# A hybrid decoder step on one core: 192 prompt tokens meet all experts in streamed blocks, 64 tokens and the sample keep gathered rows

## The chip, the cores and the metric

The kernel runs on one core of one Trainium2 chip. The metric is the device time of an execution in microseconds. The kernel before took 1012.31 us (median of three runs, 1011.79 to 1012.58).

## The reference, cut to what matters

One step of a one-layer decoder: 256 prompt tokens and 8 x 4 sample tokens go through two attention mixers and then through a channel mixer (PEER) with 16,384 single-neuron experts. Everything is float32. The change is in the channel mixer:

```python
D_MODEL, PEER_HEADS, PEER_NKEYS, PEER_TOPK = 1024, 8, 128, 16      # 128 * 128 experts
q = (xc @ w_pq).reshape(c, PEER_HEADS, 2, PEER_HALF)
s = jnp.einsum('chpd,hpkd->chpk', q, sub_keys)
sv, si = lax.top_k(s, PEER_TOPK)
cand = (sv[:, :, 0, :, None] + sv[:, :, 1, None, :]).reshape(c, PEER_HEADS, -1)
cid = (si[:, :, 0, :, None] * PEER_NKEYS + si[:, :, 1, None, :]).reshape(c, PEER_HEADS, -1)
cv, ci = lax.top_k(cand, PEER_TOPK)
eid, gate = jnp.take_along_axis(cid, ci, axis=-1), jax.nn.softmax(cv, axis=-1)
act = jax.nn.gelu(jnp.einsum('chkd,cd->chk', u_emb[eid], xc), approximate=False)
return jnp.einsum('chk,chkd->cd', gate * act, v_emb[eid])
```

Each token picks 8 x 16 = 128 experts. An expert has a row of 1,024 numbers in `peer_u` (dotted with the token) and one in `peer_v` (added to the output with weight gate x gelu). Both tables hold 16,384 rows of 4 KB.

## The kernel before, in words

The tokens are three tiles: prompt tile 0 and prompt tile 1 (128 tokens each) and the sample, tile 2 (32 tokens). Each tile runs through its heads (`heads_part`, `post`), its attention (`prompt` for tiles 0 and 1, `sample` for tile 2), the output projection (`wo_product`), the query product and the choice of experts (`query_product`, `best_keys`, `choose`). Its experts then are work in the background of the next tile's front.

Expert work is cut into slots. A slot is one chosen expert for 128 partitions: 64 tokens x 2 for a prompt tile, 32 tokens x 4 for the sample, so that the tiles have 128, 128 and 32 slots (`SLOTS`). For each slot POOL issues two indirect gathers of 128 rows of 4 KB, one of `peer_u` (L1996) and one of `peer_v` (`fetch_v`, L1978). DVE takes the 1,024-long dot products (`dot_slot`, L1453), ACT turns two slots at a time into weights (`gelu_slot`: gelu L1092, gate L1094, spread over a 64-column diagonal L1101), and PE adds weight x `peer_v` row into `acc` (`sum_slot`, through the helper `mm`, L463). Rings of seven to nine tiles hold the gathered rows.

The order is written by hand. Class `Experts` holds, for each of PE, ACT and DVE, how many slots are due: every `share(w)` or `advance(w)` in the program text adds a weight, and the engine runs the slots that are due at that point, before the next step of the front. All engines are in order, so a slot that waits holds what stands behind it. 40 slots are done while tile 0 still chooses (`EARLY`), 88 during the front of tile 1, 128 during that of tile 2, and the sample's 32 at the end. Results are normalised by `finish(t)` after `y_root(t)`. SP loads weights, cache pages (`step_pages`, `index_pages`) and stores outputs in one list.

Tile 0's token matrix for PE is `xt[0]`; `bank0` to `bank3` are four PSUM banks taken in turn; `acc` and `xr_even` fill the other four.

Of the kernel before, what the change touches and what calls it, by code (L numbers as in the profile page):

```python
# [15 lines left out]
U32 = mybir.dt.uint32  # L16
I32 = mybir.dt.int32
ALU = mybir.AluOpType
# [43 lines left out]
GELU_LAG, SUM_LAG, V_LAG = 3, 6, 5  # L62
# [5 lines left out]
CHOOSE, EARLY = 2, 40  # L68
PRELOADED = 4
SLOTS = [128, 128, 32]  # L70
BASE = [sum(SLOTS[:t]) for t in range(3)]
FRONT = 5 * W_IN + 4 * W_HEADS + 8 * W_PQ + 16 * CHOOSE

SHARES = [16 * CHOOSE, FRONT + 12 + 9 * W_PROMPT, FRONT - 8 * CHOOSE + 3 * W_INDEX + 2 * STEPS * sum(W_MID.values())]
PARTS = [[(0, 1), (1, 1), (2, 2), (4, 2), (6, 2)], [(2 * c, 2) for c in range(4)], [(0, 1), (1, 1)]]
STARTS = [[16 * h for h, _ in p] for p in PARTS]
CHOSEN = [sum(len(p) for p in PARTS[:t]) for t in range(3)]
U_GUESTS = [(24, 118), (144, sum(SLOTS) - 1)]
U_PLACE, U_LAST, U_USE = [], [], []
for n in range(sum(SLOTS)):  # L80
    places = [*range(RU), *(RU + i for i, (a, b) in enumerate(U_GUESTS) if a <= n <= b)]
    last = {p: max([m for m in range(n) if U_PLACE[m] == p], default=-1) for p in places}
    U_PLACE.append(min(places, key=lambda p: (last[p], p)))
    U_LAST.append(last[U_PLACE[n]])
    U_USE.append(U_PLACE[:n].count(U_PLACE[n]))
N_SLOTS = sum(SLOTS)
V_PLACE = [n % RV for n in range(N_SLOTS)]
V_USE = [n // RV for n in range(N_SLOTS)]
V_LAST = [n - RV for n in range(N_SLOTS)]
END_X, END_GUEST, END_ROW = N_SLOTS - 5, N_SLOTS - 4, N_SLOTS - 1  # L90
V_END = {END_X: RU, END_GUEST: RU + 1, END_ROW: U_PLACE[N_SLOTS - 7]}
for i, n in enumerate(V_END):
    V_PLACE[n], V_USE[n] = RV + i, 0
for n in (N_SLOTS - 3, N_SLOTS - 2):
    V_LAST[n] = n - RV - 2
    V_PLACE[n], V_USE[n] = V_LAST[n] % RV, V_LAST[n] // RV + 1
STAIR = 16 + 15 * 8
FIRST_SLOT = [0, EARLY, 128, 256]
# [7 lines left out]
def build(nc, inp, cst, out, scr_b, scr_d, scr_s, scr_z1, scr_z2):  # L106
    ctx = ExitStack()
    with ctx:
# [18 lines left out]
        g_q = sb("g_q_sb", [128, QL])  # L127
        g_kv = sb("g_kv_sb", [128, KVL])
# [12 lines left out]
        x = [x_b[t % 2] for t in range(3)]  # L141
        xr_odd = sb("xr_odd", [128, DM])
        more_v = sb("more_v", [128, DM])
        eid = [sb(f"eid{t}", [128, SLOTS[t]], U32) for t in range(3)]
        gate = [sb(f"gate{t}", [128, SLOTS[t]]) for t in range(3)]
# [10 lines left out]
        u_ring = [first_u[:, :], more_u[:, :]] + [rows[:, i, :] for i in range(5)] + [b[:, :] for b in x_b]  # L156
        v_ring = [more_v[:, :]] + [rows[:, i, :] for i in (5, 6, 7, 8, 9, 10, 11, 12)]
        v_ring += [u_ring[p] for p in V_END.values()]
# [3 lines left out]
        wts = sb("wts", [128, RC])  # L162

        wflat = sb("wring", [128, NW * 8 * CW])
        zflat = sb("z", [128, 2048])
# [4 lines left out]
        xt = [xt_f[:, 0:8 * P[t]].rearrange("p (k n) -> p k n", k=8) for t in range(3)]  # L170
        mix_f = sb("mix_t", [128, 1024])
        xn2 = mix_f
# [3 lines left out]
        qq_t = sb("qq_t", [QKD, NH, 128])  # L176
        qn_t = sb("qn_t", [128, HR, 128])
# [90 lines left out]
        z1_kept = xr_odd[:, 0:512]  # L268
# [13 lines left out]
        xr = [xr_even[:, :], xr_odd[:, :]]  # L282
# [29 lines left out]
        class Signal:  # L312
# [11 lines left out]
            def wait(self, eng, step):  # L324
                eng.wait_ge(self.sem, self.at[step] * self.unit)

        tiles = [0, 1, 2]
        first_in = sem("first_consts_in")
# [11 lines left out]
        y_out = sem("y_stored")  # L340
        w_in_slot = [sem(f"w_slot{i}_in") for i in range(4)]
# [30 lines left out]
        ROOTS = [("x", 0), ("x", 1), ("x", 2), ("z", 0), ("h", 0), ("z", 1), ("h", 1), ("z", 2), ("y", 0), ("h", 2), ("y", 1),  # L372
                 ("y", 2)]
        square_ready = Signal("mean_square_ready", [r for r in ROOTS if r[0] != "y"])
        root_ready = Signal("root_ready", ROOTS)
        first_pair_scored = sem("first_two_heads_of_a_quad_scored")
# [33 lines left out]
        u_in = [sem(f"u{i}_in") for i in range(RU + 2)]  # L410
        v_in = [sem(f"v{i}_in") for i in range(RV + len(V_END))]
# [3 lines left out]
        y_ready = Signal("y_ready", tiles)  # L415
        y_square = Signal("square_sums_of_sample_y_ready", [2])
# [3 lines left out]
        class Experts:  # L420
# [4 lines left out]
            def __init__(self, name, slot, lag):  # L425
                self.slot, self.lag, self.done, self.n = slot, lag, 0, 0
                self.log = handovers[name] = []

            def front(self, t):
                self.t, self.weight = t, 0  # L430

            def share(self, w):
                if self.t:
                    self.advance(w)

            def advance(self, w):
                self.weight += w
                self.log.append((self.t, w))
                assert self.weight <= SHARES[self.t], (self.t, self.weight)
                first, end = FIRST_SLOT[self.t:self.t + 2]  # L440
                until = first + (end - first) * self.weight // SHARES[self.t] - self.lag
                while self.n < until:
                    self.slot(max(self.t - 1, 0), self.n)
                    self.n += 1

            def closer(self, lag):
                first, end = FIRST_SLOT[self.t:self.t + 2]
                self.rest(self.t - 1, first + (end - first) * self.weight // SHARES[self.t] - lag - BASE[self.t - 1])

            def rest(self, t, slots=None):  # L450

                while self.n < BASE[t] + (slots or SLOTS[t]):
                    self.slot(t, self.n)
                    self.n += 1
# [14 lines left out]
        def _(pe):  # L469
# [41 lines left out]
            def sum_slot(t, n):  # L511

                if n % PAIR < PAIR - 1:
                    return
                m, u = P[t], n // PAIR
                if u == BASE[t] // PAIR:
                    if t:
                        y_ready.wait(pe, t - 1)
                    else:
                        z1_kept_done.wait(pe, 3)  # L520
                    for c in range(2 if t < 2 else 0):
                        mm(acc[0:m, c * 512:(c + 1) * 512], ident[0:m, 0:m], x[t][0:m, c * 512:(c + 1) * 512], True, False)
                    for q in range(0 if t < 2 else 4):
                        mm(acc[32 * q:32 * q + 32, 0:256], ident[0:32, 0:32], x[t][0:32, 256 * q:256 * q + 256], True, False)
                pe.wait_ge(spread_done, u + 1)
                for v in range(u * PAIR, u * PAIR + PAIR if t < 2 else 0):
                    pe.wait_ge(v_in[V_PLACE[v]], (V_USE[v] + 1) * 16)
                for c in range(2 if t < 2 else 0):
                    for j in range(PAIR):
                        g, m = WIDE * j, WIDE  # L530
                        i = mm(acc[g:g + m, c * 512:c * 512 + 512], spread[u % RD][:, j, 0:m],
                               v_ring[V_PLACE[u * PAIR + j]][:, c * 512:c * 512 + 512], False, False)
# [34 lines left out]
            def heads_part(t):  # L567

                n, r0 = P[t], ROW0[t]
                if t == 1:  # L570
                    experts.closer(4)
# [1748 lines left out]
```

## Time and profile before

| | before |
|---|---|
| median of three runs | 1012.31 us |
| profiled execution, span from first to last instruction | 1080.4 us |
| busy PE / DVE / ACT / POOL | 742.8 / 686.7 / 404.0 / 622.1 us |
| bytes moved by DMA | 381.54 MB, mean 353 GB/s |
| mean granted TensorE clock | 0.819 of 2.4 GHz |

The span is the only time that the profile gives for the profiled execution; it is 68.1 us (6.7%) above the median of the runs. A granted clock of 1.00 is 2.4 GHz and 0.50 is 1.2 GHz; a value between is the mean over a stretch. One float32 product on PE leaves two matmul records and two weight loads in the trace. Times of a window view are busy times in that window; the DMA share is the mean busy share of the core's 16 DMA engines and can read slightly over 1.

### The profile page before, as it was taken

The page shows a single profiled execution, that of the slowest core. Times are in us where ns is not written, and L with a number is a line of the kernel's source. Part 1 is how long each engine was busy: PE and PEld are TensorE (multiplying, and loading weights), DVE is VectorE, ACT ScalarE, POOL GpSimd, SP SyncE. Part 2 cuts the span into 40 slices and gives each one's busy share as a digit, 9 for nine tenths or more (in the row PEclk, how much of TensorE's full clock was granted, in tenths as well). Part 3 has the DMA queues.
Part 4 walks back from the last instruction along what each step waited for, and adds up shares of the span by engine and source line. Part 5 has one row for each costly group of instructions (what it writes and reads, how often), then busy time and mean ns, then how long its engine had stood idle before and what let it go on. Part 6 is the DMA issues. An engine that isn't in the chain of part 4 may idle for free.

```text
span 1080.4 us, 13828 instructions
## 1 busy us (share of the span) xinstructions
PE 742.8 (69%) x4217; PEld 379.1 (35%) x4217; DVE 686.7 (64%) x1725; ACT 404.0 (37%) x1154; POOL 622.1 (58%) x584
## 2 busy tenths in 40 slices
PE   8999986554798677766536768757637567765444
PEld 3575834111354435543212233323213235231111
DVE  1363776997288543698695559988974535639542
ACT  1162142332356470333223346354516742322412
POOL 0000275777667765475565656766775665667664
PEclk9999997877778899988867878877778878887656
DMA  9924699999979999999899999999998999999997
GB/s 364 331 79 184 217 349 411 411 360 377 336 252 359 348 400 412 398 379 379 278 314 325 373 388 353 391 362 362 407 412 308 411 417 416 414 411 409 382 376 270
DMA packets 122443, 381.54 MB, mean 353 GB/s; under 512 B 16026, under 2 KB 40682, under 8 KB 117122
## 3 DMA queue, kind: packets, MB, share of 16 engines
q0 software_dynamic: 83696, 304.81, 74.0%
q1 hardware_dynamic: 38578, 75.78, 19.2%
q8 instruction: 34, 0.56, 0.2%
q14 instruction: 39, 0.32, 0.1%
q10 hardware_dynamic: 96, 0.07, 0.0%
HBM read 378.16 MB, written 4.14 MB: 354 GB/s over the span
## 4 chain that ended last, share of the span: by engine, by line
PE 28%; DVE 19%; issue 17%; ACT 10%; another core or an unknown queue 9%; DMA 8%; POOL 6%; SPq 3%; ACTq 0%; POOLq 0%; DVEq 0%
PE bank L463 17%; PE acc L463 9%; DVE rows L1453 6%; DMA w_uq_sb<-in_w_uq 3%; PE bank L466 3%; POOL rows L1978 3%; DMA rows<-in_peer_v,eid 2%; POOL rows L1996 2%; ACT spread L1101 2%; ACT L1092 1%; SPq L2069 1%; DVE shared L1793 1%; DVE shared L1782 1%; ACT shared L1063 1%
## 5 line engine op out<-in xcount | busy, mean ns | idle before, releaser
L463 PE MATMUL acc<-rows,spread 128*64 128x512 f32 (+1 forms) x1124 | 329.3, 682 | 143.9 <-ACT spread L1101 51.9
L1978 POOL DMA_INDIRECT rows<-in_peer_v,eid x254 | 275.8, 1086 | 160.5 <-issue 66.6
L1996 POOL DMA_INDIRECT rows<-in_peer_u,eid x184 | 193.2, 1050 | 109.0 <-issue 54.7
L463 PEld LDWEIGHTS acc<-rows,spread 128*64 128x64 f32 (+1 forms) x1124 | 89.1, 156 | 310.3 <-issue 240.2
L1453 DVE CUSTOM_DVE_ANT_0 rows<-rows,xr_even 128x1024 f32<-128x1024 f32 x89 | 108.1, 1218 | 34.0 <-DMA rows<-in_peer_u,eid 26.4
L1453 DVE CUSTOM_DVE_ANT_0 rows<-rows,xr_odd 128x1024 f32<-128x1024 f32 x95 | 116.2, 1223 | 19.6 <-DMA rows<-in_peer_u,eid 18.8
L1101 ACT ACTIVATE spread<-wide_consts,wts 128x64 f32<-128x64 f32 (+1 forms) x288 | 83.7, 337 | 35.2 <-remote 25.0
L1996 POOL DMA_INDIRECT first_u<-in_peer_u,eid x37 | 38.2, 1032 | 101.5 <-DVE eid L1835 81.6
L463 PE MATMUL acc<-more_v,spread 128*64 128x512 f32 (+1 forms) x140 | 73.6, 695 | 18.9 <-ACT spread L1101 9.9
L1094 ACT ACTIVATE wts<-gelus,gate 128x1 f32<-128x1 f32 x288 | 69.1, 287 | 4.7
L1063 ACT ACTIVATE shared<-bank 128x512 f32<-128x512 f32 (+4 forms) x68 | 27.8, 456 | 76.3 <-remote 35.5
L1092 ACT ACT_TABLE_LOAD x42 | 53.9, 1283 | 0.7
L1092 ACT ACTIVATE gelus<-dots 128x2 f32<-128x2 f32 x144 | 28.4, 197 | 65.4 <-issue 44.0
L1978 POOL DMA_INDIRECT more_v<-in_peer_v,eid x32 | 35.5, 1108 | 19.9 <-issue 8.5
L1996 POOL DMA_INDIRECT more_u<-in_peer_u,eid x37 | 40.0, 1082 | 11.3 <-issue 11.0
L466 PE MATMUL bank<-ident,shared 128*128 128x128 f32 (+4 forms) x162 | 28.2, 292 | 26.2 <-issue 7.2
L1453 DVE CUSTOM_DVE_ANT_0 x<-x,xr_even 128x1024 f32<-128x1024 f32 x30 | 36.5, 1217 | 8.9 <-DMA x<-in_peer_u,eid 8.6
L1748 DVE MAX8 small<-ql_t 32x8 f32<-32x1056 f32 x32 | 39.9, 1248 | 0.8
L1996 POOL DMA_INDIRECT x<-in_peer_u,eid x30 | 34.3, 1144 | 9.6 <-issue 9.6
L1749 DVE MATCH_REPLACE8 ql_t<-small,ql_t 32x1056 f32<-32x1056 f32 x32 | 39.4, 1230 | 0.0
L463 PE MATMUL bank<-xt,wring 128*128 128x128 f32 x256 | 35.3, 303 | 5.1 <-issue 4.4
L463 PEld LDWEIGHTS bank<-xt,wring 128*128 128x128 f32 x256 | 34.0, 217 | 11.9 <-issue 10.9
(278 smaller groups left out, 1222.4 us busy)
## 6 DMA issues: line engine op xcount, KB each, us to landing
wring<-in_w_pq SPq DMA_DIRECT2D x12, 1024.0 KB
z<-in_w_pq SPq DMA_DIRECT2D x5, 1024.0 KB, 4.8
wring<-in_cache_ckv SPq DMA_DIRECT2D x40, 128.0 KB
rows<-in_w_in SPq DMA_DIRECT2D x2, 2048.0 KB, 15.2
rows<-in_w_pq SPq DMA_DIRECT2D x2, 2048.0 KB, 8.3
wring<-in_w_out SPq DMA_DIRECT2D x4, 1024.0 KB
wring<-in_cache_kv SPq DMA_DIRECT2D x32, 128.0 KB
rows<-in_peer_v,eid POOLq DMA_INDIRECT x254, 7.5
```

What stands on the lines that cost most here:

```text
L463: return T.matmul(o, lhsT=l, rhs=r, start=start, stop=stop, skip_group_check=True)
L466: return T.transpose(o, i, ident[0:i.shape[0], 0:i.shape[0]])
L1063: c = A.activation(o, i, ACT.Copy, scale=scale)
L1092: link(A, A.activation(gelus[:, k:k + PAIR], dots[:, k:k + PAIR], ACT.Gelu))
L1094: g = A.activation(wts[:, k + i:k + i + 1], gelus[:, k + i:k + i + 1], ACT.Copy, scale=gate[t][:, n - BASE[t] - PAIR + 1 + i:n - BASE[t] - ...
L1101: g = A.activation(spread[u % RD][:, i, 0:m], sel[:, 0:m], ACT.Copy, scale=wts[:, k + i:k + i + 1])
L1453: V.tensor_tensor_reduce(out=u, in0=u, in1=xr[j], scale=1.0, scalar=0.0, op0=ALU.mult, op1=ALU.add, accum_out=dots[:, k:k + 1]).then_inc(d ...
L1748: link(V, V.max(small[0:32, 24:32], i_s))
L1749: link(V, V.match_replace(out=i_s, in_to_replace=small[0:32, 24:32], in_values=i_s, imm_value=TAKEN))
L1782: V.max_index(index[j][:, 0:8], values[j][:, 0:8], score[j])
L1978: nc.gpsimd.indirect_dma_start(out=v_ring[V_PLACE[n]], out_offset=None, in_=inp["peer_v"], in_offset=bass.IndirectOffsetOnAxis(ap=eid[t][: ...
L1996: nc.gpsimd.indirect_dma_start(out=u_ring[U_PLACE[n]], out_offset=None, in_=inp["peer_u"], in_offset=bass.IndirectOffsetOnAxis(ap=eid[t][: ...
```

## The change

Tile 0 is split. Its first 64 tokens keep gathered slots: 128 experts x 64 tokens on 128 partitions are 64 slots (`FEW`). The other 64 tokens of tile 0 and all 128 of tile 1 (`MANY` = 192) are multiplied with all experts. The experts are 128 blocks of 128; SP streams a turned copy of `peer_u` (`peer_ut`) and `peer_v`, 512 KB each per block. PE multiplies the block with the 192 tokens (`dots_of_blocks`), ACT takes gelu of two blocks at a time (`gelu_blocks`), DVE multiplies with a dense gate matrix (`weigh`), and PE adds the block's rows into two accumulators (`sums_of_blocks`). The sample keeps 32 gathered slots, now last on POOL.

The dense gate matrix holds 32 blocks at a time (`g_part`, four parts in two buffers). It is made in 24 chunks of 8 tokens per part: for each token a one-hot matrix of its experts' first key times the gate (`one_i`, by DVE) and one of the second key (`one_j`, by POOL; for the odd chunks of the first part by DVE), multiplied on PE (`turn_weights`) and copied out by ACT (`keep_weights`). The chosen indices and gates are first turned so that experts lie on partitions (`turn_chosen`, `keep_chosen`).

The schedule becomes one list of items: 32 pairs of gathered slots of tile 0, 48 pairs of blocks, then 16 pairs of blocks alternating with 16 pairs of the sample's slots. 8 items are due while tile 0 chooses, 20 during the front of tile 1, 4 in the heads of tile 2; then come the first 24 chunks, and 48 pairs of blocks during the sample stage. SP runs the same list two items ahead for the loads. `y` of tile 0 leaves in two halves.

```diff
-SLOTS = [128, 128, 32]
+FEW, ALL = 64, 128
+MANY = 128 + ALL - FEW
+N_SLOTS = FEW + NB * NT
+BLOCKS = 128
+PBLOCKS, PCHUNKS = 32, MANY // 8
+MIX_FROM = 48
+ITEMS = [("s", u) for u in range(FEW // PAIR)] + [("d", d) for d in range(MIX_FROM)]
+for d in range(MIX_FROM, BLOCKS // PAIR):
+    ITEMS += [("d", d), ("s", FEW // PAIR + d - MIX_FROM)]
+D0, N_ITEMS = FEW // PAIR, len(ITEMS)
+FIRST_ITEM = [0, 8, 28, D0, D0 + MIX_FROM]
+def chunks_of(d):
+    p, k = d // (PBLOCKS // PAIR), d % (PBLOCKS // PAIR) - 4
+    return range(PCHUNKS * (p + 1) + 2 * k, PCHUNKS * (p + 1) + 2 * k + 2) if k >= 0 and p < BLOCKS // PBLOCKS - 1 else range(0)
...
+            def turn_weights(c):
...
+                b = take(pe, ("g", c))
+                for k in range(8):
+                    i = mm(b[:, 32 * k:32 * k + 32], one_j[c % 2][:, k, :], one_i[c % 3][:, k, :])
+                full(i, ("g", c))
+            def dots_of_blocks(d):
+                b = take(pe, ("u", d))
+                for j in range(PAIR):
+                    n = PAIR * d + j
+                    pe.wait_ge(du_in[n % 4], (n // 4 + 1) * 16)
+                    u = bias_u[0] if n % 4 == 3 and n >= KEYS_TO else dense_u[n % 4]
+                    for k in range(8):
+                        i = mm(b[:, MANY * j:MANY * j + MANY], u[:, 128 * k:128 * k + 128], xd[:, k, :], k == 0, k == 7)
+                full(i, ("u", d))
+            def sums_of_blocks(d):
+                pe.wait_ge(weights_ready, d + 1)
+                for j in range(PAIR):
+                    n = PAIR * d + j
+                    pe.wait_ge(dv_in[n % 4], (n // 4 + 1) * 16)
+                    v = bias_u[1] if n % 4 == 3 and n >= KEYS_TO else dense_v[n % 4]
+                    w = acts[d % 4][:, MANY * j:MANY * j + MANY]
+                    for q in range(2):
+                        mm(acc_d[64 * q:64 * q + 64, :], w[:, 0:64], v[:, 512 * q:512 * q + 512], False, False)
+                    for q in range(2):
+                        i = mm(acc_1[:, 512 * q:512 * q + 512], w[:, 64:192], v[:, 512 * q:512 * q + 512], False, False)
+                i.then_inc(dense_done, 1)
+            def step(n):
...
+                if kind == "d":
+                    for c in chunks_of(k):
+                        turn_weights(c)
+                    dots_of_blocks(k)
+                sums(n - BEHIND)
...
+            def gelu_blocks(d):
+                if d >= 4:
+                    act.wait_ge(dense_done, d - 3)
+                b = ready(act, ("u", d))
+                A.activation(acts[d % 4], b[:, 0:PAIR * MANY], ACT.Gelu).then_inc(acts_ready, 1)
+                act.wait_ge(acts_ready, d + 1)
+                drained(A.activation(small[:, 41:42], small[:, 14:15], ACT.Copy), ("u", d))
...
+                link(V, V.tensor_tensor(o, free(iota[:, PBLOCKS * p:PBLOCKS * p + 1], (0, 8), (1, PBLOCKS)),
+                                        free(t[:, 0, 0:1], (1, 8), (0, PBLOCKS)), ALU.is_equal))
+                V.tensor_tensor(o, o, free(t[:, 2, 0:1], (1, 8), (0, PBLOCKS)), ALU.mult).then_inc(one_i_ready, 1)
+                if c < PCHUNKS and c % 2:
...
+                    V.tensor_tensor(one_j[1], free(iota[:, 0:1], (0, 8), (1, 128)), free(t[:, 1, 0:1], (1, 8), (0, 128)),
+                                    ALU.is_equal).then_inc(one_j_first, 1)
...
+                dve.wait_ge(acts_ready, d + 1)
+                V.tensor_tensor(acts[d % 4], acts[d % 4], g_part[p % 2][:, PAIR * MANY * k:PAIR * MANY * (k + 1)],
+                                ALU.mult).then_inc(weights_ready, 1)
...
                 else:
+                    experts.rest(D0)
+                    for c in range(PCHUNKS):
+                        turn_weights(c)
+                    start_sums_of_tile_1()
+                    experts.front(3)
                     sample()
...
+            fetch(0, FEW)
...
+            for c in range(BLOCKS // PBLOCKS * PCHUNKS):
+                k = c % PCHUNKS
+                if c < PCHUNKS and c % 2:
+                    continue
+                if c >= 2:
+                    ready(pool, ("g", c - 2))
...
+                for q in range(8):
+                    i = nc.gpsimd.tensor_scalar(one_j[c % 2][:, q, :], iota, t[:, q:q + 1], None, ALU.is_equal)
+                i.then_inc(one_j_ready, 1)
+            fetch(FEW, N_SLOTS)
...
+                if n >= 4:
+                    ready(sp, ("u", (n - 4) // PAIR))
...
+                load(o, inp["peer_ut"][n, :, :], du_in[n % 4])
...
+                if n >= 4:
+                    sp.wait_ge(dense_done, (n - 4) // PAIR + 1)
...
+                load(o, inp["peer_v"][128 * n:128 * n + 128, :], dv_in[n % 4])
```

## Rows read from the trace of the kernel before

**Rows 1.** The page: busy time of each engine, and the queue of the gathers.

```profile
PE 742.8 (69%) x4217; PEld 379.1 (35%) x4217; DVE 686.7 (64%) x1725; ACT 404.0 (37%) x1154; POOL 622.1 (58%) x584
...
q0 software_dynamic: 83696, 304.81, 74.0%
```

**Rows 2.** Windows: stretch, length; busy PE, PEld, DVE, ACT, POOL; clock, DMA share, GB/s.

```profile
0.00:109.00 109.00, 101.82 (x564) 61.45 (x565) 39.75 (x116) 33.07 (x88) 3.34 (x8) 0.98 0.67 241
109.00:245.00 136.00, 96.60 (x563) 54.42 (x561) 108.97 (x391) 43.54 (x117) 86.19 (x79) 0.87 0.92 348
245.00:445.00 200.00, 151.22 (x691) 88.88 (x692) 107.19 (x219) 89.40 (x247) 128.63 (x123) 0.84 0.95 357
445.00:550.00 105.00, 63.79 (x355) 35.08 (x356) 89.22 (x342) 31.25 (x91) 64.43 (x61) 0.82 0.95 350
550.00:602.00 52.00, 26.65 (x119) 10.71 (x117) 31.69 (x80) 14.67 (x55) 32.96 (x29) 0.76 0.96 331
602.00:893.00 291.00, 194.66 (x1139) 81.78 (x1137) 209.49 (x354) 139.60 (x376) 192.54 (x175) 0.79 1.00 381
893.00:985.00 92.00, 63.68 (x503) 32.31 (x499) 53.16 (x150) 26.49 (x88) 58.44 (x53) 0.82 1.02 413
985.00:1080.40 95.40, 44.36 (x298) 14.43 (x294) 47.22 (x76) 26.00 (x95) 55.61 (x60) 0.63 0.92 353
```

**Rows 3.** Windows, expert sums alone (tile spread): busy PE, PEld, ACT; clock, DMA, GB/s.

```profile
245.00:445.00 200.00, 63.84 (x224) 17.96 (x225) 17.42 (x60) 0.84 0.95 357
445.00:550.00 105.00, 38.12 (x138) 10.29 (x140) 9.00 (x31) 0.82 0.95 350
...
602.00:893.00 291.00, 98.72 (x344) 25.93 (x344) 26.42 (x90) 0.79 1.00 381
893.00:985.00 92.00, 36.24 (x120) 9.60 (x122) 8.22 (x28) 0.82 1.02 413
```

**Rows 4.** Windows, dot products alone (L1453, two instructions per dot): busy DVE; clock, DMA, GB/s.

```profile
109.00:245.00 136.00, 47.63 (x80) 0.87 0.92 348
245.00:445.00 200.00, 68.85 (x114) 0.84 0.95 357
445.00:550.00 105.00, 34.47 (x58) 0.82 0.95 350
550.00:602.00 52.00, 16.34 (x28) 0.76 0.96 331
```

**Rows 5.** Timeline of PE: start, length; a query product, and two expert sums of one moment.

```profile
119.67 7.41 PE L463 MATMUL bank<-xt,rows 128*128 128x128 f32 x64
...
154.92 0.59 PE L463 MATMUL acc<-more_v,spread 128*64 128x512 f32 x1
154.93 0.59 PE L463 MATMUL acc<-rows,spread 128*64 128x512 f32 x1
```

**Rows 6.** Timeline of weight loads: first and tenth of a run of 512-column products.

```profile
139.91 0.19 PEld L463 LDWEIGHTS acc<-rows 128*128 128x128 f32 x1 [0.24 <-issue]
...
143.77 0.19 PEld L463 LDWEIGHTS acc<-rows 128*128 128x128 f32 x1 [0.24 <-issue]
```

**Rows 7.** Groups on DVE by shape: busy us, mean ns of one; idle before.

```profile
L1499 DVE TENSOR_TENSOR shared<-shared 128x256 f32<-128x256 f32 x4 | 1.7, 425 | 0.1
...
L1696 DVE COPY shared<-bank 128x128 f32<-128x128 f32 x8 | 2.3, 291 | 22.1 <-remote 18.4 <-PE bank L463 3.7
```

**Rows 8.** Groups on POOL by shape: busy us, mean ns of one; idle before.

```profile
L1996 POOL DMA_INDIRECT rows<-in_peer_u,eid x184 | 193.2, 1050 | 109.0 <-issue 54.7 <-DVE dots L1453 45.4 <-PE bank L463 8.8
...
L2299 POOL MEMSET const-float32-0.0<- 128x1 f32 x1 | 0.1, 98 | 0.2 <-issue 0.2
```

**Rows 9.** Groups on ACT by shape: busy us, mean ns of one; idle before.

```profile
L1092 ACT ACT_TABLE_LOAD x42 | 53.9, 1283 | 0.7
...
L1063 ACT ACTIVATE shared<-bank 128x512 f32<-128x512 f32 x32 | 16.8, 597 | 18.0 <-remote 14.4 <-PE bank L466 3.6
```

**Rows 10.** Timeline of DVE: the root of tile 0's result in `finish`.

```profile
579.59 0.16 DVE L1506 RECIPROCAL small<-small 128x1 f32<-128x1 f32 x1 [9.69 <-ACT small L1129]
```

More of the change, by code:

```diff
@@ L79 @@
[L79 to L88, printed above, removed]
@@ L442, in advance, with rest @@
+            def rest(self, until):
                 while self.n < until:
[L443 to L453, printed above, removed]
+                    self.step(self.n)
@@ L542, in _ @@
+            experts = Experts("PE", step, 0)
             share = experts.share
@@ L1387, in _ @@
                 else:
+                    experts.rest(D0)
+                    for c in range(PCHUNKS):
+                        keep_weights(c)
+                    experts.front(3)
                     sample()
@@ L1467, in _, with step @@
+            def step(n):
+                kind, k = ITEMS[n]
+                if n == NORM_0A:
+                    finish("0a")
+                if kind == "s":
+                    for j in range(PAIR):
+                        dot(PAIR * k + j)
+                weigh(n - 1)
+                for c in chunks_of(ITEMS[n + 1][1]) if n + 1 < N_ITEMS and ITEMS[n + 1][0] == "d" else []:
+                    one_hots(c)
+            experts = Experts("DVE", step, 0)
             share = experts.share
@@ L2110, in _, with load_gain @@
+            def load_gain(o, m):
+                w = DM * m // 128
+                for q in range(128 // m):
+                    load(o[m * q:m * q + m, :], bass.AP(inp["g_final"].tensor, inp["g_final"].offset + w * q, [[0, m], [1, w]]), g_fin_in)
             load(relb, inp["rel_bias"], hot_in)
@@ new lines, in _ @@
+            experts.front(3)
+            experts.rest(D0 + 2)
+            for e in range(3):
+                if e:
+                    ready(sp, ("is", e - 1, 1))
+                    step_pages("m", e)
+                share(W_INDEX)
+            for e in range(STEPS):
+                for i in range(2):
+                    share(W_MID["m"])
+                ready(sp, ("mso", e))
+                if e + 3 < STEPS:
+                    step_pages("m", e + 3, step_ids(e + 3) if e + 3 >= SUB else None)
+                if e == 4:
@@ L2211, in _ @@
+            sp.wait_ge(sample_scored, 2)
+            load(gains[1], bcast(inp["g_final"], DM), g_fin_in)
+            load_gain(gains["0b"], 64)
+            load_gain(gains[2], 32)
+            experts.rest(N_ITEMS)
+            for n in range(BLOCKS - 4, BLOCKS):
+                load_v(n)
+            for t in (1, "0b", 2):
+                output(t)
+            sp.wait_ge(y_out, 16 * 9)
             sp.wait_ge(stored_z, 240)
+            assert handovers["SP"] == [w for w in handovers["PE"] if w[0] == 3]
```

620 lines of the change are left out of this document (380 added, 240 removed).

## The prediction, made before the changed kernel was run

> **What bounds the kernel now.** I read the page first, for what is busy over the whole span: no engine is above 69%, and the queue of the gathers alone keeps the 16 DMA engines busy for 74% [rows 1]. Then I cut the span where the program changes stage (109 us: first keys of tile 0; 245: heads of tile 1; 445: its first keys; 550: its last gates; 602: sample; 893: its output projection; 985: its last gates) and read each stretch [rows 2]. From 109 us on, the DMA engines are at 0.92 to 1.02 of their time while PE is at 46 to 76%. Only the first 109 us look otherwise: PE is busy for 101.82 of them. So the gathers set the pace: 288 slots of 2 x 512 KB are 302 MB of the queue's 304.81 MB [rows 1]. POOL, busy for 192.54 of 291 us in the sample stage, is second. PE has room, but a number to keep in mind is how much: 1080 minus 743 us, 338 us [rows 1].
>
> **What the change removes.** 192 of 288 slots: 201 MB of gathers, 384 POOL issues, 192 dots. It adds 128 x 2 x 512 KB = 134 MB of plain loads. DMA has 67 MB less to move of 381.5, which at the 381 GB/s of the sample stage [rows 2] is 176 us. That is the gain on the old bound, and it would be the whole story if PE had the room.
>
> **What it adds on PE.** The unit is a record; a product has two. Nine steps between the weight loads of 512-column products take 143.77 - 139.91 = 3.86 us, 0.429 us each [rows 6]; 64 records of 128 columns, each with its own 128x128 weights, take 7.41 us, 0.115 each [rows 5]. Both are at full clock, and a line through them gives 0.167 us for 192 columns. Two products with 64 columns of weights start 0.01 us apart and run side by side [rows 5]. So a block costs:
> - dots: 8 products of 192 columns, 16 x 0.167 = 2.67 us;
> - sums: the two 64-column products side by side are 2 records' time, the two 128-column ones 4: 6 x 0.429 = 2.57 us.
>
> 5.24 us a block, 671 us for 128. Already this is twice the room that PE has now.
>
> A gate chunk is 8 products of only 32 columns with fresh 128x128 weights. By the line a record would take 0.037 us if the weight load hid; no such record stands in the rows. The upper end is the 0.115 of a 128-column record with the same load. I take 0.115, since the load and not the columns should set the pace there: 1.84 us a chunk, 96 chunks 177 us (at 0.037, 57).
>
> **The sum, stage by stage, in the profiled execution's time.** Dense work cannot start before tile 1's experts are chosen, as the gates and the token matrix need them.
> - To 245 us: 16 dots instead of 40, at 47.63/40 = 1.19 us [rows 4] 28.6 us less on DVE, whose idle there is 136 - 109 = 27 us [rows 2]. Gain 28.6 to 55.6; I take the middle, 42: 203 us.
> - Tile 1's front, 305 us now: 86 slots' dots [rows 4] become 40. DVE: 196.4 - 103.3 + 47.6 = 141 us. PE: 215.0 - 102.0 + 20 pairs of 2.25 (362 records, 8 a pair, took 102.0 [rows 3]) = 158. Transfers: 0.95 x 305 less 46 slots of 1.05 MB at 355 GB/s (136 us) = 154. Lower end 158; upper end 305 - 46 x 1.19 = 250, where nothing but DVE's dots goes. Its steps depend on each other, so I take 200, near the middle: 403 us.
> - Heads of tile 2: 52 us now, less the wait of 9.69 for tile 0's result [rows 10], which moves into the sample stage behind dense items, and less 14 dots (16.34 [rows 4]), plus 8 dots: 36. 439 us.
> - First 24 chunks, with nothing of the sample beside them: PE 44 us. DVE: 48 x 0.425 [rows 7] + 12 of 1,024 elements at a dot's 1.2 = 35. POOL: 12 x 8 compares of 128 elements. The rows show no arithmetic on POOL; the ends are 0.098 (a memset of one column) and 1.05 (issuing a gather) [rows 8]. I take 0.3, by the same shape on DVE, 0.291 [rows 7]. POOL waits for the chunk two back, so building and multiplying alternate: 2.4 + 1.84 + some 0.6 of handovers, 12 times: 58 us (44 to 130). Dense work starts at 497 us.
> - From there PE: 671 + 72 chunks 132 + the sample's own PE work, 258.3 - 135.0 = 123 us at clock 0.8 [rows 2, 3], 99 at full clock + the sample's 32 slots, whose four 256-column products run side by side, 4 x 0.21 a pair, 14. Total 916 us. With no wait at all 916; at the 93% of the first stretch [rows 2] 981. I take 950: 1447 us.
> - Result: one root and product cost 9.69 + 1.3 us [rows 10]; three overlap in part. 11 to 33, I take 15: 1462 us.
>
> Against the profiled span of 1080.4 that is +382. The span is 68.1 us above the median. I assume that the excess lies where transfers set the pace and scale only the part before 497 us by 0.937: 466 + 950 + 15 = **1431 us** (all scaled 1370, nothing scaled 1462). I call it 1430.
>
> A rule against POOL's part: [rows 8] leave its price open by a factor of ten. The Trainium skill (GPSIMD Engine Reference, section 4.1) advises against elementwise work on GpSimd: about half as fast as VectorE with two inputs, near its rate with one. At twice 0.291 the first chunks would take 86 us in place of 58 and the time 1457. No run here shows it yet.
>
> **Costed at nothing, and the cover.** For a pair of blocks ACT needs a gelu of 384 columns (under 0.6 us), at most two table loads of 1.28 [rows 9] and two chunk copies, some 4 us; DVE a product of 384 (under 1.2) and four one-hots of 0.425 [rows 7], 3 us. Both lie beside 10.5 us of PE. If they were late, each wait would stand in PE's order in front of all sample work, as the sums wait for `weights_ready`; two items lie between, 20 us. SP's loads are 2.1 MB a pair, 200 GB/s against 381 reached [rows 2]; SP waits there for dots two pairs back, and the page loads and projection weights of the sample queue behind that wait, three steps ahead of use. In the last 16 items 2 slots come on top: 4.2 MB in 11.3 us, 370 GB/s, close to the 353 to 413 of the last stretches: 0 to 9 us. POOL starts the sample's gathers only after its last one-hot, at pair 47; pairs 48 and 49 cover the first landing. The outputs of tile 0 and the loads of `g_final` move on SP, a few transfers behind dense loads, covered by the same pairs.
>
> **The rivals.**
> 1. POOL is slow. If a compare costs the 1.05 us of an issue, the first chunks take 130 us (+72), and two chunks 17 us where their pair of blocks needs 10.5 + 3.7: 36 pairs x 2.6 = +95. About 1600 us. For it: no row has POOL arithmetic; against: 128 elements are little. It decides from 0.9 us on.
> 2. The clock sags. Now it is granted at 0.98 where PE is busy for 93%, 0.63 where it is for 46% [rows 2]. If waits of the sample's chain let the dense stretch swing between 1.2 and 2.4 GHz as the whole kernel does now, at 0.82, PE's 916 us become 1117: 1600 to 1640. Against: dense items are long and independent. The Trainium skill (TensorE: Matmul & The Clock Gate, Part 1) has the array at half clock unless activity releases it, and by that rule gaps between bursts bring this case about.
> 3. The other side: dense products overlap as the 64-column ones do, or cost one record. Dots, sums and chunks at half price: 402 + 99 + 14 = 515 us, near what the transfers allow (168 MB of experts and, by the loads in the code, some 30 of pages and weights: 520 us at 381 GB/s): 466 + 520 + 15 = 1001 us, 1.1% faster. It decides from 0.52 of my price on. Against: the 128-column weights of [rows 5, 6] run one record after another, without exception.
>
> **How the numbers follow.** Forecast 0.79, POOL 0.10, clock 0.08, the other side 0.03. The forecast's own range, since the ends of the stages before dense work (427 to 632 us together) hardly fall all to one side, is 1320 to 1540; to hold 8 in 10 with the slow cases I go to 1310 and 1600. A measurement tells some 0.2%. Faster has 0.02, the same 0.01 (the other side falling short), slower 0.97.
>
> **What would show it.** Right: PE busy over 90% from some 450 to 500 us to the end with a clock near 1; records of 192 columns every 0.167 us and 512 every 0.429; the DMA share near a half; 235 MB of expert bytes. The steps are wrong if dense work starts before 400 or after 580 us, if a chunk's record is far from 0.115, or if POOL's compares show before PE's waits. A span below 1200 us would break the price of a record, on which all rests.

## The result, and the profile after

The changed kernel takes **1599.33 us** (median of four executions, 1598.61 to 1602.31) beside 1012.16 us before: a ratio of 1.580, 95% interval 1.577 to 1.582. The prediction said 1430, with a range from 1310 to 1600: the side and the cause came out, and the time lies 0.7 us inside the end of the range, 169 us above the forecast. The profiled execution has a span of 1600.5 us and took 1602.31. In three experiments below with unused products, one or two executions lie 60 to 70 us from the others at another mean granted clock; they are named there.

The page of the profile, in the lines that answer to [rows 1]:

```profile
PE 1435.5 (90%) x8083; PEld 990.9 (62%) x8083; DVE 578.2 (36%) x1566; ACT 389.8 (24%) x905; POOL 618.9 (39%) x872
...
q1 hardware_dynamic: 76226, 211.65, 37.7%
q0 software_dynamic: 28400, 103.46, 17.9%
```

The gathers' queue has fallen from 74% of the DMA engines' time [rows 1] to 17.9%, and with the streamed tables all queues stay near 56%. PE is busy for 1435.5 us where it was for 743.

The windows by stage, as [rows 2] (tile 1's heads begin at 202 us, its last choice is at 428, the one-hots of the first chunk begin at 466, the dense blocks follow from 585 to 1590):

```profile
245.00:440.00 195.00, 131.63 (x689) 86.98 (x688) 111.86 (x389) 71.02 (x161) 49.41 (x52) 0.79 0.63 212
440.00:466.00 26.00, 18.30 (x86) 8.49 (x85) 10.87 (x22) 9.98 (x41) 14.87 (x16) 0.68 0.87 317
466.00:585.00 119.00, 87.10 (x393) 83.32 (x390) 36.57 (x71) 14.68 (x26) 73.71 (x102) 0.50 0.08 29
585.00:1130.00 545.00, 540.52 (x3096) 383.22 (x3096) 165.99 (x300) 137.17 (x268) 238.38 (x395) 0.96 0.47 160
1130.00:1360.00 230.00, 222.25 (x1430) 162.71 (x1430) 52.50 (x169) 36.03 (x74) 105.97 (x170) 0.95 0.48 176
1360.00:1590.00 230.00, 230.00 (x1152) 135.73 (x1150) 49.31 (x86) 32.72 (x119) 75.00 (x71) 0.99 0.83 306
```

From 585 us on PE is busy for 992.8 of 1005 us, as forecast, with the DMA share near a half up to 1360. The surprise is the stretch before it: 119 us in which the DMA engines stand still (0.08), PE is busy for 87 us, and the clock is at its lower level, 1.2 GHz. Against the prediction, stage by stage:

| step | predicted | after | difference |
|---|---|---|---|
| tile 1's heads begin | 203 | 202 | -1 |
| tile 1's front | 200 | 226 | +26 |
| heads of tile 2, to the first chunk | 36 | 38 | +2 |
| first 24 chunks | 58 | 119 | +61 |
| dense blocks, to the last product | 950 | 1005 | +55 |
| result | 15 | 10.5 | -4.5 |
| from the profile to the runs (the factor 0.937) | -31 | -1 | +30 |

The differences add up to +168.5. The experiments take the four large ones in turn. Inside the dense blocks, a pair of blocks and two chunks read like this at full clock (timeline of PE):

```profile
651.07 1.08 PE L506 MATMUL acc<-more_v,w_uq_sb 128*64 128x512 f32 x4
652.08 1.99 PE L506 MATMUL xr_even<-more_v,w_uq_sb 128*128 128x512 f32 x4
653.99 1.08 PE L506 MATMUL acc<-x,w_uq_sb 128*64 128x512 f32 x4
655.00 1.98 PE L506 MATMUL xr_even<-x,w_uq_sb 128*128 128x512 f32 x4
656.82 0.38 PE L509 MATMUL bank<-ident,shared 128*128 128x128 f32 x2
...
659.43 1.97 PE L506 MATMUL bank<-w_uq_sb,g_fin_sb 128*128 128x32 f32 x16
661.24 1.95 PE L506 MATMUL bank<-w_uq_sb,uk_t 128*128 128x32 f32 x16
```

Read the starts, since the ends are modelled and overlap. The sums of two blocks run from 651.07 to 656.82, 5.75 us where 2 x 2.57 = 5.14 were forecast. A chunk takes 1.81 (1.84 forecast). The dots of a pair take 5.40 (5.34 forecast), where no chunk stands right before them. But behind two chunks they look like this:

```profile
709.77 1.95 PE L506 MATMUL bank<-w_uq_sb,uk_t 128*128 128x32 f32 x16
711.56 4.53 PE L506 MATMUL bank<-xd,first_u 128*128 128x192 f32 x16
715.92 2.76 PE L506 MATMUL bank<-xd,more_u 128*128 128x192 f32 x16
718.62 1.08 PE L506 MATMUL acc<-more_v,w_uq_sb 128*64 128x512 f32 x4
```

The same 16 records take 4.36 us and then 2.70: for some microseconds the clock is at the lower level, with no gap in the work. After the low clock of the first chunks there are 13 such episodes, some 4 to 10 us each. Twelve stand at two chunks in a row, the last of them at 1370 us behind the last two chunks. One has no chunks near it: it begins at 1152 us, while PE waits 3.35 us for DVE between products of the sample:

```profile
1153.88 0.48 PE L509 MATMUL bank<-ident,shared 128*128 128x128 f32 x1 [3.35 <-DVE shared L1928]
```

### The profile page after: what moved, and what is told of

Same layout as the page of the kernel before. It is cut to its first block, busy times and chain, and to the rows that moved or that the text cites. A ratio compares the mean times of both kernels' runs of the same rounds, so it can differ in the third digit from the quotient of the medians.

```text
span 1600.5 us, 21795 instructions
## 1 busy us (share of the span) xinstructions
PE 1435.5 (90%) x8083; PEld 990.9 (62%) x8083; DVE 578.2 (36%) x1566; ACT 389.8 (24%) x905; POOL 618.9 (39%) x872
## 3 DMA queue, kind: packets, MB, share of 16 engines
q0 software_dynamic: 28400, 103.46, 17.9%
## 4 chain that ended last, share of the span: by engine, by line
PE 79%; DVE 5%; POOL 5%; DMA 5%; ACT 4%; issue 1%; SPq 0%; DVEq 0%; POOLq 0%; ACTq 0%
PE bank L506 49%; PE xr_even L506 16%; PE acc L506 13%; POOL g_fin_sb L2228 4%; DMA w_uq_sb<-in_w_uq 2%; PE bank L509 2%; DMA rows<-in_peer_v,eid 2%; DMA wring<-in_w_pq 1%; ACT L1209 1%; DVE shared L1988 0%; DVE shared L2002 0%; SPq L2236 0%; ACT L1371 0%; DVE rows L1624 0%; DVE shared L1999 0%
## 5 line engine op out<-in xcount | busy, mean ns | idle before, releaser
L2228 POOL TENSOR_SCALAR g_fin_sb<-wide_consts,g_q_and_g_kv 128x128 f32<-128x128 f32 x256 | 167.0, 671 | 221.6 <-PE bank L506 221.6
L506 PE MATMUL bank<-w_uq_sb,g_fin_sb 128*128 128x32 f32 x768 | 113.3, 307 | 32.8 <-POOL g_fin_sb L2228 31.9
L506 PEld LDWEIGHTS bank<-w_uq_sb,g_fin_sb 128*128 128x128 f32 x768 | 110.3, 227 | 46.4 <-POOL g_fin_sb L2228 35.1
L506 PE MATMUL bank<-w_uq_sb,uk_t 128*128 128x32 f32 x768 | 119.1, 316 | 0.0
L2228 POOL TENSOR_SCALAR uk_t<-wide_consts,g_q_and_g_kv 128x128 f32<-128x128 f32 x192 | 115.9, 629 | 0.0
L506 PEld LDWEIGHTS bank<-w_uq_sb,uk_t 128*128 128x128 f32 x768 | 115.2, 237 | 0.0
L506 PE MATMUL bank<-xd,x 128*128 128x192 f32 x512 | 108.3, 374 | 0.0
L2187 POOL DMA_INDIRECT rows<-in_peer_v,eid x88 | 83.2, 946 | 50.8 <-PE acc L506 29.8
L506 PEld LDWEIGHTS bank<-xd,x 128*128 128x128 f32 x512 | 99.3, 221 | 4.8 <-issue 4.8
L506 PE MATMUL bank<-xd,first_u 128*128 128x192 f32 x512 | 98.9, 350 | 0.0
```

The source lines that it names most:

```text
L506: return T.matmul(o, lhsT=l, rhs=r, start=start, stop=stop, skip_group_check=True)
L2187: nc.gpsimd.indirect_dma_start(out=v_ring[V_PLACE[n]], out_offset=None, in_=inp["peer_v"], in_offset=bass.IndirectOffsetOnAxis(ap=eid[:, a ...
L2228: i = nc.gpsimd.tensor_scalar(one_j[c % 2][:, q, :], iota, t[:, q:q + 1], None, ALU.is_equal)
```

## The experiments

Times are medians of four executions unless said otherwise. The ratios are to the kernel before on the same chip; a difference between two kernels is taken between their medians. The medians of the kernel before beside them lie between 1012 and 1014 us.

### Half of every dense dot

```diff
-                    for k in range(8):
-                        i = mm(b[:, MANY * j:MANY * j + MANY], u[...], xd[:, k, :], k == 0, k == 7)
+                    for k in range(4):
+                        i = mm(b[:, MANY * j:MANY * j + MANY], u[...], xd[:, k, :], k == 0, k == 3)
```

> Left out: in every dense dot product the products of the second 512 of 1,024 model columns (8 of 16 records a block). Theory (PE's price of float32 products sets the time from 585 us on): 128 blocks x 8 records x 0.168 us = 172 us less, of which some 5 come back in the last 32 blocks, where the transfers are at 0.83 of their time: 1430 us. Rival (transfers, or the order of gelu, weigh and sums, set the pace): 1590 to 1600 us, with PE's busy share falling instead. In between (1450 to 1480): the narrow gate products then weigh more and the clock is lower.

Measured: 1453.41 us (1449.52 to 1458.82), ratio 1.436 (1.430 to 1.441): 146 us less. In its profile the first chunks end at 585 us, as in the changed kernel, and the last product at 1443:

```profile
585.00:1443.00 858.00, 838.46 (x4664) 524.60 (x4668) 267.61 (x555) 206.07 (x462) 420.74 (x635) 0.94 0.64 231
```

PE is still busy for 838 of 858 us, so nothing else took over: the rival falls, and **PE's work sets the time**. Of the 172 us, 26 are missing, and most are found where the expectation's last sentence looked. The dots' own busy time fell by 156.5 us, from 374.4 to 217.9, and not by 172: the dots that run at the lower clock behind the chunks are a larger part of what is left (granted clock 0.94, before 0.96). PE's idle time rose by 7 us: PE now waits 4.8 us for rows of `peer_v` and 2.5 us for DVE's weighing, where the changed kernel has no such waits.

### Narrow sums first

```diff
+                pair = []
                 for j in range(PAIR):
...
+                    pair.append((w, v))
                     for q in range(2):
                         mm(acc_d[64 * q:64 * q + 64, :], w[:, 0:64], v[...], False, False)
+                for w, v in pair:
                     for q in range(2):
                         i = mm(acc_1[:, 512 * q:512 * q + 512], w[:, 64:192], v[...], False, False)
```

> Same work, other order: in the sums of a pair of blocks the 64-column products of both blocks come first, then the 128-column ones, so that the width of the weights changes twice in a pair and not four times. Theory (a change of width leaves a weight load in the open, and this is the excess of 2.92 us a block over 2.57): half of the changes goes, 64 pairs x 0.35 us = 22 us less: 1577 us. Rival (the excess has to do with other things, the bank of the accumulator or reading the weights): 1599 us.

Measured: 1579.01 us (1573.01 to 1581.63), ratio 1.560 (1.556 to 1.565): 20 us less. The timeline of PE:

```profile
649.31 1.08 PE L506 MATMUL acc<-more_v,w_uq_sb 128*64 128x512 f32 x4
650.22 1.03 PE L506 MATMUL acc<-x,w_uq_sb 128*64 128x512 f32 x4
651.17 1.99 PE L506 MATMUL xr_even<-more_v,w_uq_sb 128*128 128x512 f32 x4
653.00 1.88 PE L506 MATMUL xr_even<-x,w_uq_sb 128*128 128x512 f32 x4
654.71 0.38 PE L509 MATMUL bank<-ident,shared 128*128 128x128 f32 x2
```

5.40 us in place of 5.75 for the same products, and the second group of 128-column products starts 1.71 us before what follows it: four times the 0.429 of [rows 6], the price without the excess. So the excess belongs to the **change of width**. The accumulator changes at the same places; a change of accumulator without one of width was not run, but the step from one half of an accumulator to the other lies inside those 1.71 us and costs nothing. In the changed kernel's trace one sees why, in the weight loads (PEld) at such a change:

```profile
1588.12 0.30 PEld L506 LDWEIGHTS xr_even<-bias_d,w_uq_sb 128*128 128x128 f32 x2 [0.81 <-issue]
1588.13 1.98 PE L506 MATMUL xr_even<-bias_d,w_uq_sb 128*128 128x512 f32 x4
1588.66 0.19 PEld L506 LDWEIGHTS xr_even<-bias_d,w_uq_sb 128*128 128x128 f32 x1 [0.24 <-issue]
```

The first load of the new width starts with the product and not ahead of it, after 0.81 us of pause; within a width the next load starts while the product before it still runs, as in [rows 6].

### DVE alone makes the first one-hots

```diff
-                if c < PCHUNKS and c % 2:
-                    pe.wait_ge(one_j_first, c // 2 + 1)
+                if c < PCHUNKS:
+                    pe.wait_ge(one_j_first, c + 1)
...
-                if c < PCHUNKS and c % 2:
+                if c < PCHUNKS:
                     if c >= 2:
                         ready(dve, ("g", c - 2))
-                    V.tensor_tensor(one_j[1], ...
+                    V.tensor_tensor(one_j[c % 2], ...
...
-                if c < PCHUNKS and c % 2:
+                if c < PCHUNKS:
                     continue
```

In the changed kernel POOL and PE take turns (timeline, then PE's waits from 466 to 585 us):

```profile
481.42 3.62 PE L506 MATMUL bank<-w_uq_sb,g_fin_sb 128*128 128x32 f32 x16 [2.62 <-POOL g_fin_sb L2228]
...
484.85 3.60 PE L506 MATMUL bank<-w_uq_sb,uk_t 128*128 128x32 f32 x16
...
485.14 5.88 POOL L2228 TENSOR_SCALAR g_fin_sb<-wide_consts,chosen_of_tile_turned 128x128 f32<-128x128 f32 x8 [3.77 <-PE bank L506]
```

```profile
PE bank L506 <- POOL g_fin_sb L2228: 31.9, 12, 3.1
```

> Same work: the one-hot of the second key of the first 24 chunks is made by DVE alone, not by POOL and DVE in turn. Theory (POOL's 5.9 us a chunk and PE's two chunks at half clock alternate, and so make the first part 120 us long): DVE needs 2.1 us a chunk, PE 3.45 at half clock, so the part takes 24 x 3.45 = 83 us: 1562 us. Rival 1 (the clock is low there because PE waits): with the waits gone PE needs 1.84 us and DVE's 2.1 sets the pace, 50 us: 1530 us. Rival 2 (the copies out or the banks set the pace): 1599 us.

Measured: 1564.03 us (1559.13 to 1571.81), ratio 1.547 (1.540 to 1.554): 35 us less, the theory's number. Its windows before and over the first chunks, and PE's timeline:

```profile
450.00:466.00 16.00, 14.71 (x64) 7.13 (x64) 6.69 (x12) 5.14 (x23) 6.24 (x7) 0.50 1.04 391
466.00:550.00 84.00, 84.00 (x388) 82.76 (x387) 47.48 (x79) 14.71 (x24) 4.73 (x9) 0.50 0.09 33
```

```profile
480.01 3.60 PE L506 MATMUL bank<-w_uq_sb,g_fin_sb 128*128 128x32 f32 x16
483.42 3.60 PE L506 MATMUL bank<-w_uq_sb,uk_t 128*128 128x32 f32 x16
```

The waits are gone: PE is busy for 84.00 of 84 us. Yet a chunk still takes 3.41 us and the granted clock reads 0.50 all through, so rival 1, which had the low clock come from the waits in this part, falls as well. The clock is at 0.50 already when the part begins; what the chunks show here is that they do not raise it. At 1.81 the 24 chunks would take 43 us: once POOL's 35 us are gone, 38 us are lost to the clock.

### One chunk before the dots, one between them

```diff
-                    for c in chunks_of(k):
-                        turn_weights(c)
                     dots_of_blocks(k)
...
+                chunks = list(chunks_of(d))
+                if chunks:
+                    turn_weights(chunks[0])
                 b = take(pe, ("u", d))
                 for j in range(PAIR):
+                    if j and chunks:
+                        turn_weights(chunks[1])
```

> Same work, other order: of the two gate chunks of an item the second is multiplied between the dots of its two blocks, not right behind the first. Theory (two chunks in a row, 16 products of 32 columns, are what lets the clock fall for 3 to 10 us at a time between 690 and 1360 us): the episodes go, granted clock over 0.98 from 585 us on, some 30 us less: 1569 us. Rival 1 (one chunk of 8 products is enough): the episodes stay, 1599 us. Rival 2 (the episodes come from waits that only happen to lie there): 1599 us, and the dips move to other places than the chunks.

Measured: 1568.39 us (1566.66 to 1572.46), ratio 1.550 (1.546 to 1.555): 31 us less, for the same products in another order. The stretch with chunks, in the changed kernel and then in this one (whose window holds 71 records more), and this one's timeline:

```profile
591.00:1360.00 769.00, 756.77 (x4510) 543.69 (x4509) 218.00 (x469) 172.43 (x340) 338.39 (x554) 0.96 0.48 166
```

```profile
588.00:1340.00 752.00, 739.76 (x4581) 522.88 (x4581) 221.15 (x473) 175.56 (x345) 348.34 (x564) 1.00 0.50 175
```

```profile
704.28 1.87 PE L506 MATMUL bank<-w_uq_sb,g_fin_sb 128*128 128x32 f32 x16
705.98 2.85 PE L506 MATMUL bank<-xd,first_u 128*128 128x192 f32 x16
708.66 1.87 PE L506 MATMUL bank<-w_uq_sb,uk_t 128*128 128x32 f32 x16
710.37 2.85 PE L506 MATMUL bank<-xd,more_u 128*128 128x192 f32 x16
```

The twelve episodes at the chunks are gone: granted clock 1.00, and the dots behind a chunk take 2.68 us, not 4.36. Two chunks in a row let the clock fall; one between wider products did not in this kernel. Rival 1 falls. Rival 2 falls for those twelve, as PE's waits in this stretch are the same in both (12.2 us); it holds for the thirteenth, which stays: behind the same wait for DVE, now 3.36 us, the clock is at 0.50 from 1127 to 1133 us.

### Places for gathered rows up to slot 56

```diff
-CLEAR, GUEST = 40, 24
+CLEAR, GUEST = 56, 24
```

In the changed kernel, between 202 and 428 us, PE and POOL waited for this (the longest waits of PE, then of POOL):

```profile
PE acc L506 <- DMA rows<-in_peer_v,eid: 37.9, 7, 12.6
```

```profile
POOL more_u L2206 <- DVE dots L1624: 53.7, 5, 23.8
```

> Same work: the places of gathered rows that the gate matrix takes over are used up to slot 56, not 40, so that the slots of tile 1's front keep eight places. Theory (that front takes 226 us and not 200 as POOL waits for one of three places, and PE for the rows that POOL could not ask for: 37.9 us in 7 waits): most of the 26 us goes: 1575 us, the last choice of tile 1 near 404 us. Rival (DVE's dots or the chain of the front set its pace): 1595 to 1600 us. Against both: the first copies of the gate matrix wait for a later slot, up to 5 us.

Measured: 1574.00 us (1570.52 to 1577.04), ratio 1.551 (1.548 to 1.555): 25 us less. The last step of tile 1's choice, in the timelines of DVE of the changed kernel and of this one:

```profile
427.81 0.15 DVE L2063 COPY small<-small 128x1 f32<-128x1 f32 x1
```

```profile
405.83 0.15 DVE L2063 COPY small<-small 128x1 f32<-128x1 f32 x1
```

So the theory holds: 22 of the 26 us came from the **three places** that slots 40 to 63 were left. The waits are a chain: POOL may not ask for the next `peer_u` rows before DVE has used a place, the request for the `peer_v` rows stands behind that one in POOL's order, and PE holds the front of tile 1 until they land. With eight places PE has no waits for these rows left in tile 1's front.

### The four edits together

> The four edits that keep the work (narrow sums first, DVE's one-hots in the first part, split chunks, places up to slot 56) together. If each acts on a part of its own: 1599 - 20 - 35 - 31 - 24 = 1489 us. If two of them paid for the same time (split chunks and narrow sums both touch the clock), 1500 to 1520. Still far above the kernel before: PE's own work is then some 1,330 us.

Measured: 1485.83 us (1483.61 to 1486.23), ratio 1.465 (1.462 to 1.467): 113.5 us less, where the four alone gave 20.3 + 35.3 + 30.9 + 25.3 = 111.8. So they hardly overlap. It is the fastest of the changed kernels that do only the work that is needed, and 46% slower than the kernel before.

### Unused wide products in the first chunks

The low clock of the first 24 chunks is left. Four kernels put products of 256 columns between them, whose results go to the unused half of the bank:

```diff
                 for k in range(8):
                     i = mm(b[:, 32 * k:32 * k + 32], one_j[c % 2][:, k, :], one_i[c % 3][:, k, :])
+                    if c < PCHUNKS and k == 7:
+                        i = mm(b[:, 256:512], ident[:, :], xd_f[:, 0:256])
```

With two a chunk the condition is `k % 4 == 3`, with three `k in (2, 4, 7)`.

> Added to the kernel in which DVE makes all one-hots of the first 24 chunks (1564 us): behind each of these chunks one product of 256 columns whose result is not used (two records, 0.44 us at full clock). There PE is busy without a gap at a granted clock of 0.50, so waits are not what keeps it low. Theory A (32-column products leave the clock low, and a wide one between them lets it rise): a chunk takes 1.84 + 0.44 = 2.3 us, 55 instead of 82: 1537 us. Theory B (the clock stays low): 3.45 + 0.88 = 4.3 us, 104 us: 1586 us.

Measured: 1585.94 us (1577.52 to 1588.26), ratio 1.561 (1.556 to 1.566): 22 us more than without the products, theory B. The windows of its first chunks:

```profile
490.00:520.00 30.00, 30.00 (x128) 28.74 (x128) 14.04 (x22) 4.29 (x7) 0.00 (x0) 0.50 0.00 1
```

> As the kernel with one unused product of 256 columns behind each of the first 24 chunks, but with two, one behind each four products. Theory A: 1.84 + 0.88 = 2.7 us a chunk, 65 instead of 82: 1547 us. Theory B (the clock stays low): 3.45 + 1.76 = 5.2 us, 125 us: 1607 us. If the kernel with one product stays low and this one rises, it is the share of wide work that decides.

Measured, five executions: 1536.96, 1541.77 and 1543.98 us at a mean granted clock of 0.934 to 0.936, and 1604.67 and 1608.05 us at 0.895. These are the two theories' numbers, 1547 and 1607, from one and the same kernel; the profiled execution was the one of 1608.05, with a clock of 0.50 before and over the first chunks, which begin at 464 us:

```profile
450.00:464.00 14.00, 12.55 (x56) 6.27 (x54) 5.93 (x12) 5.13 (x23) 4.45 (x5) 0.50 1.04 393
464.00:585.00 121.00, 121.00 (x475) 112.52 (x474) 47.04 (x79) 14.10 (x23) 2.63 (x5) 0.50 0.06 20
```

The ratio of the three is 1.518 (1.515 to 1.522).

> The kernel with the four edits together (1486 us) and two unused products of 256 columns in each of the first 24 chunks. With that much wide work the earlier kernel ran at either level of the clock: three executions near 1541 us, two near 1606. So here too: at full clock 24 x (3.41 - 2.72) = 17 us less, 1469 us; at half clock 24 x 1.76 = 42 us more, 1528 us. Rival (the level is set by what went before the part, and that is another thing here): all executions at one of the two.

Measured, six executions: five from 1464.14 to 1467.14 us and one of 1525.61; ratio of the five 1.446 (1.442 to 1.450). Again both numbers (1469, 1528) were met, but the full clock more often. The profile is of one at full clock; its window over the first chunks:

```profile
440.50:503.00 62.50, 62.50 (x474) 60.04 (x472) 47.22 (x77) 14.17 (x23) 1.05 (x2) 1.00 0.15 51
```

The four edits alone, where the same part begins at the same time:

```profile
440.50:443.00 2.50, 2.50 (x23) 2.50 (x24) 2.27 (x4) 0.48 (x1) 0.00 (x0) 1.00 1.06 321
445.00:520.00 75.00, 75.00 (x353) 75.00 (x353) 43.75 (x73) 13.41 (x22) 3.23 (x6) 0.50 0.08 29
```

Without the wide products the part begins at full clock, falls during its second chunk and stays low to its end: 79 us. With them it stays at full clock: 64 us. So **more work makes the kernel faster** in five of six executions: 1466 us against 1486, with 48 products that nobody uses.

> As the kernel with two unused wide products a chunk, but with three. If the share of wide work decides the level: full clock in all executions, 24 x (3.41 - 3.16) = 6 us less than 1486: 1480 us, with a granted clock near 1.0 over the first 24 chunks. If it is chance, or set by what went before: half clock in some executions, 24 x 2.64 = 63 us more: 1549 us.

Measured, six executions: five from 1473.09 to 1476.95 us and one of 1544.60; ratio of the five 1.455 (1.451 to 1.459). A third product costs 10 us and does not make the full clock certain. The first reading of the expectation (full clock in all executions) falls. What tips an execution to one side or the other is **open**. The three profiles with two or three wide products a chunk keep the level of the part's first microseconds: 1.00 in these two kernels, 0.50 in the one of 1608.05 us. That would fit a level set by what went before the part, but no kernel has a profile at both levels.

## Why the prediction was right in its side and short in its size

**The range held by luck.** The range without the rivals, 1320 to 1540 us, was missed by 59 us. It leaned on errors that would not all fall to one side, and the four large ones did: front, first chunks, dense blocks and the factor. The end at 1600 was drawn for a slow POOL and a sagging clock; both came, each in part, and the time lies 0.7 us inside.

**PE's price for float32 products** held. The forecast had 0.167 us for a record of 192 columns and measured were 0.169 (5.40 us for 32); a chunk took 1.81 for 1.84; the chunk's price was taken from the weight load and not from the columns, and that was the right end. PE is the bound from 585 us on, which half the dots showed. Rival 3, half price, is out. But all three signs that the prediction named against its own steps came: dense work began after 580 us, at 585; POOL's compares stood before PE's waits; and in the first part a record of a chunk took 0.213 us (3.41 for 16), far from 0.115.

**Tile 1's front, 200 us, was mis-sized by 26.** The working took off what the removed slots had cost and chose the middle. It did not count how many places the remaining slots were left: `CLEAR` stood in the code, and the rings' size was no term of the sum. Places up to slot 56 gave back 25 us.

**The first 24 chunks, 58 us, are the worst step: 119.** The cycle of POOL and PE was right in form, 2.4 + 1.84 + 0.6 per two chunks. Both numbers in it were off. POOL's compare was taken at 0.3 us and took 0.67 and 0.63 (two groups of POOL by shape, most of them from later parts); in the first part eight took 5.88 us:

```profile
L2228 POOL TENSOR_SCALAR g_fin_sb<-wide_consts,g_q_and_g_kv 128x128 f32<-128x128 f32 x256 | 167.0, 671 | 221.6 <-PE bank L506 221.6
L2228 POOL TENSOR_SCALAR uk_t<-wide_consts,g_q_and_g_kv 128x128 f32<-128x128 f32 x192 | 115.9, 629 | 0.0
```

That is inside the bounds of [rows 8], 0.098 and 1.05, and off the value chosen from DVE's [rows 7]. A shape that fits on another engine was no price for this one. And PE's 1.84 became 3.41, for which the sum had no term: the clock was a rival only for the dense stretch, by way of waits. By the cycle, an estimate: 12 x (5.88 - 2.4) = 42 us are POOL's and 12 x (3.41 - 1.84) = 19 us the clock's. Rival 1 decides from 0.9 us a compare and was never near from 585 us on: there POOL waited 430.6 us for PE, and PE not at all for POOL. POOL cost time in the first part alone. DVE in its place gave back 35 us.

The Trainium skill (GPSIMD Engine Reference, section 4.1) advises against elementwise work on GpSimd, which the trace bears out, but calls its speed with one input roughly line-rate. Here DVE made the same 8 x 128 compares in one instruction of 1.22 us, and POOL in eight, 5.88 us in all; how much of that is a fixed price of each instruction, no run here tells.

**The dense blocks, 950 us, came out at 1005.** By start-to-start times: dots 64 x 5.40 = 346 for 342; sums 64 x 5.75 = 368 for 329; 72 chunks 130 for 132; the episodes of low clock 31 (what splitting the chunks gave back), for nothing; all else, the sample's work and waits, 130 (what is left of 1005) for 147. Together +55. The sums' 39 us are the changes of width; the term took 0.429 us from [rows 6], a row in which the width never changes, and of [rows 5] the pairs of one width. Half the changes gave back 20.

**The clock's rival** had the right fear and, in the main, the wrong cause. It priced a swing over the whole dense stretch through gaps in the sample's chain; PE had 12 us of gaps there, and one episode of 13 stands behind one. The others came within full work, at the chunks. The loss is 31 us there and, by the cycle above, some 19 in the first part, about 50 of the 169 that the forecast is short.

The Trainium skill (TensorE: Matmul & The Clock Gate, Part 1) lets the clock follow how busy the array has been. The profile's busy share and the clock do not go together here: the share was 100% over 84 us at 1.2 GHz.

**The factor 0.937 was a wrong step, +30.** The profiled execution of before was 68 us above the runs, and the prediction took 31 us off the part before 497 us. After, the span and that execution's own time differ by 1.8 us. DVE's first choice of keys, ahead of which the change alters little, began at 109.6 us before and at 107.7 after, 2% earlier and not 6%. The unscaled forecast for the start of tile 1's heads was met (203 and 202), but its gain was the middle of 27 us, so that match may be chance. Why that one execution of before was longer is open; the executions of before beside these experiments lie between 1010 and 1019 us.

**The result**, 15 us, took 10.5, below its lower end of 11. **Costed at nothing** and borne out: gelu, weighing and copies beside PE (DVE 36%, ACT 24% busy), the loads up to 1360 us, and the last 16 items, whose range was 0 to 9 us: PE has no idle time there (230.00 of 230) at a DMA share of 0.83.

The four edits and the unused products bring the kernel to 1466 us. An order of the same work that would come under 1012 is not in sight: PE's dots, sums and chunks alone take 346 + 329 + 96 x 1.81 = 849 us at full clock, and up to 466 us PE was busy with other things for 354 us at mean clocks of 0.63 to 0.95, by an estimate some 307 at full clock: 1156 us together.

## What to carry to other kernels

Price the work on the engine that gains it, record by record, before counting the bytes saved on the one that loses it: here 65 MB less for DMA stood against 849 us of new work for PE at full clock. When a step gets a rate from a row, ask what that row leaves out: the weights' width never changed in it, the clock was full, the shape ran on another engine, the ring had more places. Long runs of products with few columns are worth breaking up with wider ones: here the same products in another order were 31 us faster.

## What was not expected of the hardware

- PE busy without a gap for 84 us at a granted clock of 0.50, in products of 32 columns with fresh 128x128 weights. One chunk of eight such products between 192-column products left the clock at 1.00 over 752 us; two in a row did not (0.96). A part of 24 chunks that began at full clock was at 0.50 from its second chunk on.
- One kernel at two levels of the clock: 1537 to 1544 us in three executions, 1605 and 1608 in two.
- A change between 64 and 128 columns of weights cost about 0.15 us (0.61 us over four changes in a pair of blocks), as the first load of the new width did not run under the product before it.
- POOL's compare of 128x128 float32 numbers took 0.63 to 0.67 us; DVE's of eight times as many 1.22 us.
